# Strassen's scheme for the gate and up projections of a two-layer hybrid encoder on one NeuronCore

## The chip, the cores and the metric

One core of one Trainium2 chip runs the whole inference step as one program. The metric is device time in microseconds (us) of one execution; three runs of the kernel before gave 3285.12, 3286.22 and 3287.9 us. The core's engines run side by side and meet at semaphores: TensorE (PE, with PEld for its weight loads), VectorE (DVE), ScalarE (ACT), GpSimd (POOL) and SyncE (SP, which here issues weight loads). DMAs are issued from SP's and ACT's queues.

## The reference, cut to what matters

D is 1024, the feed-forward width D_FF is 2816, and 1024 prompt tokens and 32 sample tokens go together as N = 1056 columns. Each of the two layers ends in the part that the change touches:

```python
def _swiglu(h, wg, wu, wd):
    a = jnp.einsum('btd,df->btf', h, wg)
    b = jnp.einsum('btd,df->btf', h, wu)
    return jnp.einsum('btf,fd->btd', jax.nn.silu(a) * b, wd)
...
    xp = xp + g1p[:, None] * mp          # mp: the mixer's output projection
    hp = _modulate(xp, norm_ffn[l], sh2p, sc2p)
    xp = xp + g2p[:, None] * _swiglu(hp, w_ffn_gate[l], w_ffn_up[l], w_ffn_down[l])
```

`_modulate` is an RMSNorm with a gain, times (1 + scale), plus a shift. The other outputs (keys, values, states, of both layers) come from stages that the change leaves alone. All of it is float32.

## The kernel before, in words

Activations lie with features on the 128 partitions and tokens along the free dimension: `x` is [128, 8, 1056]. A float32 product is made of three passes (`passes`, L106 to L110): each operand is split into an upper part of fewer bits (`hi`, written as fp32r) and the rest (`lo`), and w_hi·hi, w_hi·lo and w_lo·hi are accumulated in PSUM. Who splits: GpSimd the weights (a CAST, L272, and a subtraction TENSOR_TENSOR, L274, over 2048 columns for a unit of two 128-wide weight blocks), ScalarE and VectorE the activations.

`trunk_phase` runs once for each layer. Its list of units (`TrunkPlan`) is: 4 "out" units (the mixer's output projection), then for each of six parts (4, 4, 4, 4, 3, 3 blocks of 128 features of D_FF) its "up" units and 4 "down" units, and in layer 0 at the end 8 "z" and 4 "tok" units, the next layer's input projection. An up unit is one block of gate and the same block of up. Every unit but tok goes over three thirds of 352 tokens, and for each third accumulates two PSUM banks (a = 0, 1) over k = 8 blocks (nk for down), three passes each: 24 matmuls a bank, 144 an up unit, 72 or 54 a down unit. There are three pairs of banks, reused in turn (`accumulator_free`).

After an up step, ScalarE takes Silu of the gate's bank (L357), VectorE multiplies by the up bank (L462), ScalarE writes the upper half (L359) and VectorE the rest (L466) to `inner`, from which the down units of the same part read. VectorE adds a down or out step to `x` (`residual`, L444). After the last out unit the norm of the feed-forward input is computed third by third, by `sums` on TensorE (L324), `roots` on ScalarE (L394) and `norm` on VectorE: a reciprocal (L482), then 8 tiles (L489), each shifted and split by ScalarE (L404) and `lower_half` (L473); the first up unit waits for them tile by tile (`h_ready`).

The order on each engine is written out by hand, by the list `events` and the loops over it; each engine runs its instructions in order. Weights come through two `raw` buffers: SP waits until GpSimd has split unit u - 2 before it loads unit u (the wait at L241), and GpSimd waits until TensorE has finished unit u - 2 before it writes w[u % 2].

## Time and profile before

| | us |
|---|---|
| median of three runs | 3286.22 |
| the profiled execution's own time | 3287.2 |
| its span in the trace | 3285.4 |
| TensorE busy | 3012.2 |
| VectorE, GpSimd, ScalarE busy | 1412.1, 846.2, 728.4 |
| trunk of layer 0, from the first out matmul to the last tok matmul | 933.0 to 2103.4 |
| trunk of layer 1, from the first out matmul to the last down matmul | 2389.2 to 3256.0 |

The profile is of one execution. Matmuls overlap in the pipe, so a matmul's own duration (322 ns at 352 columns) is twice the distance from one to the next (159 ns); the distance is what a matmul costs. Busy spans of GpSimd are rough.

### The profile page before, as it was taken

The numbers are of one execution on the slowest core, as the hardware profiler recorded it, in microseconds if no ns is written. First come the engines' busy times: TensorE is split into PE (matmuls) and PEld (weight loads), VectorE is DVE, ScalarE is ACT, GpSimd is POOL, SyncE is SP. The second block draws the span as 40 slices with busy tenths as digits, with TensorE's granted clock in tenths as the row PEclk, the third lists the DMA queues.
The fourth block names the chain that finished last, engine by engine and source line by source line (L and its number), as shares of the span: only waits on it lengthen the run. The fifth ranks groups of instructions, "written<-read, shape, count | busy, mean of one in ns | idle before, by whom it ended". The sixth has DMA issues, their size and how long they took to land. (4 is left out here: it accounts for less than half of the span.)

```text
span 3285.4 us, 55023 instructions
## 1 busy us (share of the span) xinstructions
PE 3012.2 (92%) x23527; PEld 2803.3 (85%) x23527; DVE 1412.1 (43%) x2792; ACT 728.4 (22%) x1659; POOL 846.2 (26%) x415
## 2 busy tenths in 40 slices
PE   6999999894769999999999999899689999999996
PEld 3859999562669999999999899766488999999996
DVE  5489999454647222122224400155347212122126
ACT  2341211453422100101002211266323010100102
POOL 1111222562422232222332222000032232232230
PEclk8999999996889999999999999999899999999998
DMA  5626662624051011110111222332120111011011
GB/s 200 220 78 217 224 226 81 210 81 135 3 203 39 27 58 46 46 58 26 49 54 53 76 99 75 117 137 102 45 101 27 52 39 65 26 58 46 28 56 61
DMA packets 135011, 290.89 MB, mean 89 GB/s; under 512 B 19032, under 2 KB 84336, under 8 KB 127152
## 3 DMA queue, kind: packets, MB, share of 16 engines
q1 hardware_dynamic: 104464, 244.87, 22.1%
q10 hardware_dynamic: 30304, 42.49, 3.6%
q8 instruction: 187, 3.06, 0.4%
q14 instruction: 56, 0.46, 0.0%
HBM read 244.51 MB, written 55.70 MB: 91 GB/s over the span
## 5 line engine op out<-in xcount | busy, mean ns | idle before, releaser
L108 PE MATMUL tr_acc<-tr_h_hi,tr_w_hi 128*128 128x352 f32 x2880 | 939.1, 326 | 69.4 <-POOL tr_w_lo L274 41.6
L109 PE MATMUL tr_acc<-tr_h_lo,tr_w_hi 128*128 128x352 f32 x2880 | 928.2, 322 | 0.0
L110 PE MATMUL tr_acc<-tr_h_hi,tr_w_lo 128*128 128x352 f32 x2880 | 927.5, 322 | 0.0
L108 PEld LDWEIGHTS tr_acc<-tr_h_hi,tr_w_hi 128*128 128x128 f32 x2880 | 544.1, 189 | 76.8 <-POOL tr_w_lo L274 42.1
L272 POOL CAST tr_w_hi<-tr_raw 128x2048 fp32r<-128x2048 f32 (+2 forms) x112 | 169.4, 1513 | 1543.8 <-PE tr_acc L110 1408.0
L109 PEld LDWEIGHTS tr_acc<-tr_h_lo,tr_w_hi 128*128 128x128 f32 x2880 | 545.7, 189 | 0.7
L110 PEld LDWEIGHTS tr_acc<-tr_h_hi,tr_w_lo 128*128 128x128 f32 x2880 | 544.2, 189 | 0.0
L274 POOL TENSOR_TENSOR tr_w_lo<-tr_raw,tr_w_hi 128x2048 fp32r<-128x2048 f32 (+2 forms) x112 | 405.5, 3620 | 9.0
L462 DVE TENSOR_TENSOR tr_value<-tr_value,tr_acc 128x352 f32<-128x352 f32 x132 | 68.7, 520 | 722.9 <-ACT tr_value L357 722.9
L444 DVE SCALAR_TENSOR_TENSOR x<-tr_acc,mod,x 128x352 f32<-128x352 f32 x448 | 194.6, 486 | 364.0 <-PE tr_acc L110 361.2
L108 PE MATMUL tr_acc<-tr_inner_hi,tr_w_hi 128*128 128x352 f32 x1056 | 342.2, 324 | 0.0
L109 PE MATMUL tr_acc<-tr_inner_lo,tr_w_hi 128*128 128x352 f32 x1056 | 339.4, 321 | 0.0
L110 PE MATMUL tr_acc<-tr_inner_hi,tr_w_lo 128*128 128x352 f32 x1056 | 338.9, 321 | 0.0
L357 ACT ACTIVATE tr_value<-tr_acc 128x352 f32<-128x352 f32 x132 | 61.2, 464 | 1185.8 <-PE tr_acc L110 1185.7
L560 DVE TENSOR_SCALAR_CACHE_REDUCE f_q<-score,choose_trial 128x384 bf16<-128x384 f32 (+6 forms) x224 | 242.2, 1145 | 1.1
L1488 DVE CUSTOM_DVE_ANT_0 pc_prob<-pc_dots,pc_bias 128x640 f32<-128x640 f32 (+4 forms) x128 | 83.2, 651 | 347.1 <-POOL pc_bias L1323 267.3
L108 PE MATMUL f_acc<-h_hi,f_w_hi 128*128 128x352 f32 x600 | 202.5, 337 | 7.2 <-DVE h_lo L1102 7.2
L109 PEld LDWEIGHTS tr_acc<-tr_inner_lo,tr_w_hi 128*128 128x128 f32 x1056 | 199.1, 189 | 0.4 <-issue 0.2
L108 PEld LDWEIGHTS tr_acc<-tr_inner_hi,tr_w_hi 128*128 128x128 f32 x1056 | 198.8, 188 | 0.4 <-DVE x L444 0.3
L110 PEld LDWEIGHTS tr_acc<-tr_inner_hi,tr_w_lo 128*128 128x128 f32 x1056 | 198.6, 188 | 0.0
L110 PE MATMUL f_acc<-h_hi,f_w_lo 128*128 128x352 f32 x600 | 193.4, 322 | 0.0
L109 PE MATMUL f_acc<-h_lo,f_w_hi 128*128 128x352 f32 x600 | 193.4, 322 | 0.0
(279 smaller groups left out, 4164.9 us busy)
## 6 DMA issues: line engine op xcount, KB each, us to landing
f_ada_w<-in_w_ada_dram SPq DMA_DIRECT2D x48, 1024.0 KB, 5.2
tr_raw<-in_w_gate_dram SPq DMA_DIRECT2D x44, 512.0 KB, 3.7
tr_raw<-in_w_up_dram SPq DMA_DIRECT2D x44, 512.0 KB, 4.5
tr_raw<-in_w_down_dram SPq DMA_DIRECT2D x64, 256.0 KB, 2.9
f_raw<-in_w_dram SPq DMA_DIRECT2D x24, 512.0 KB, 6.9
out_z_dram<-f_stage ACTq DMA_DIRECT2D x60, 176.0 KB, 1.9
out_z_dram<-tr_value ACTq DMA_DIRECT2D x48, 176.0 KB, 2.0
tr_raw<-in_w_out_dram SPq DMA_DIRECT2D x16, 512.0 KB, 8.3
```

The lines of the kernel that those rows point to most:

```text
L108: pe.matmul(out, w_hi, hi, start=start, stop=False)
L109: pe.matmul(out, w_hi, lo, start=False, stop=False)
L110: return pe.matmul(out, w_lo, hi, start=False, stop=stop)
L272: pool.tensor_copy(hi, own).then_inc(w_hi, 1)
L274: pool.tensor_tensor(lo, own, hi.bitcast(F32), ALU.subtract).then_inc(w_ready, 1)
L357: act.activation(value[n % 3][:], acc[s % 3][0][:, 0:THIRD], ACT.Silu).then_inc(gated, 1)
L444: done = dve.scalar_tensor_tensor(out=x[:, k, lo:hi], in0=acc[s % 3][a][:, lo - THIRD * t:hi - THIRD * t], scalar=gate[:, k, of:of + 1], i ...
L462: dve.tensor_tensor(value[n % 3][:], value[n % 3][:], acc[s % 3][1][:, 0:THIRD], ALU.mult).then_inc(multiplied, 1)
L560: last = dve.tensor_scalar(marks[n % 2][0:p, 0:width], score[0:p, at:at + width], bound(p, j), 0.0, compare, ALU.add, accum_out=count[0:p, ...
L1488: dve.tensor_tensor_reduce(prob[2 * (u % 3) + hd][:, 0:n], dots[hd][:, at_dots(u):at_dots(u) + n], add, -DH ** -0.5, 3.0e38, ALU.add, ALU. ...
```

## The change

The 8 products of a unit (2 halves of the tokens, 2 halves of the 1024 input features, gate and up) become 7 (Strassen's scheme in Winograd's form), with sums and differences of halves ahead and behind. Blocks of tokens are a quarter wide (264) and a half is 528. Per layer:

- Out units go over four blocks of 264 columns. Norm, shift and split of the feed-forward input go by halves of 528. Seven moving operands M1 to M7 of [128, 4, 528] are kept, each split into hi and lo (`quad`): three are quarters of the normed input, four are its differences (`full`).
- An up unit is seven products of 24 matmuls of 264 columns: 168. The first two units run as a pair, product by product, while the moving operands are being made, and compute M1 twice: 192 matmuls each.
- GpSimd makes four sums of the weight quarters (`combine`) and splits seven quarters of 512 columns (`factor`, `split`) for each up unit. Split weights go through a ring of six slots of a quarter unit.
- ScalarE and VectorE put gate and up together from the products (nine VectorE instructions and four of ScalarE, all of 528 columns, for each unit from the third on), the gated values are stored to DRAM, and after the last up unit all down units run; their inputs are loaded again and split (`part_half`, `part_rest`), two parts ahead at most.
- There are four pairs of PSUM banks.

```diff
+UP_ORDER = [M1, M2, M6, M5, M7, M3, M4]
+PAIR_ORDER = [M1, M2, M3, M5, M6, M7, M4]
+RING, RING_WIDE = 6, 8
...
-        self.units = [("out", j, 0, KD) for j in range(KD // 2)]
-        first, self.last_up = 0, {}
-        for nk in TRUNK_PARTS:
-            self.units += [("up", f, first, KD) for f in range(first, first + nk)]
+        self.units = [("out", j, 0, KD) for j in range(KD // 2)] + [("up", f, 0, KD) for f in range(KF)]
+        for first, nk in zip(PART_FIRST, TRUNK_PARTS):
             self.units += [("down", j, first, nk) for j in range(KD // 2)]
...
+            def split(u, n, own):
+                i = plan.slot_no[u, n]
+                hi, lo = slot(u, n)
+                width = own.shape[-1]
+                slot_free(i)
+                pool.tensor_copy(hi[:, 0:width], own).then_inc(w_hi, 1)
+                pool.wait_ge(w_hi, i + 1)
+                pool.tensor_tensor(lo[:, 0:width], own, hi[:, 0:width].bitcast(F32), ALU.subtract).then_inc(w_ready, 1)
+
+            def combine(u):
...
+                pool.tensor_tensor(w_sum[b][:], r21, r22, ALU.add).then_inc(combined, 1)
+                pool.wait_ge(combined, 4 * f + 1)
+                pool.tensor_tensor(r21, r11, r21, ALU.subtract).then_inc(combined, 1)
+                pool.wait_ge(combined, 4 * f + 2)
+                pool.tensor_tensor(r11, w_sum[b][:], r11, ALU.subtract).then_inc(combined, 1)
+                pool.wait_ge(combined, 4 * f + 3)
+                pool.tensor_tensor(r12, r12, r11, ALU.subtract).then_inc(combined, 1)
+                pool.wait_ge(combined, 4 * f + 4)
...
+            def half_sums(h):
+                pe.wait_ge(out_summed, add_no(UP_FIRST - 1, 2 * h + 1, 1) + 1)
...
+            def accumulate(u, n, product, out, start, stop):
+                f = u - UP_FIRST
+                pe.wait_ge(w_ready, plan.slot_no[u, n] + 1)
+                for b in range(2):
+                    for k in range(KH):
+                        if f == 0 and b == 0:
+                            pe.wait_ge(quad_ready, KH * QUADS[product] + k + 1)
...
+                        done = passes(pe, out[:, b, 0:BLOCK], w_hi_v, w_lo_v, upper, lower, start and k == 0, stop and k == KH - 1)
...
+            for j in range(UP_FIRST):
+                outputs(j)
+            pair_first(0)
+            half_sums(1)
+            pair_again(0)
+            pair_again(1)
+            pair_first(1)
+            for n in range(1, 7):
+                for f in range(2):
+                    pair_product(n, f)
+            for f in range(2, KF):
+                up_products(f)
...
+            def store_inner(f):
+                b, n = f % 2, f // 2
+                act.wait_ge(right_done[b], n + 1)
+                act.dma_start(io["inner"][f][:, HALF:N], flat(values_of(f)[1])).then_inc(right_stored[b], 16)
...
+            def unit_tile(h, k):
+                for lo, hi, s in HALF_SPANS[h]:
+                    own = slice(lo - HALF * h, hi - HALF * h)
+                    done = dve.scalar_tensor_tensor(out=full[2 * (k // KH) + h][:, k % KH, own], in0=x[:, k, lo:hi],
+                                                    scalar=up_gain[:, k, s:s + 1], in1=flat(rstd_half[h])[:, own],
+                                                    op0=ALU.mult, op1=ALU.mult)
...
+            def lower(product, k):
+                dve.wait_ge(quad_hi, KH * QUADS[product] + k + 1)
+                dve.tensor_tensor(quad[product][1][:, k], source[product][:, k], quad[product][0][:, k].bitcast(F32),
+                                  ALU.subtract).then_inc(quad_ready, 1)
+
+            def difference(n, k, out, first, second):
+                dve.tensor_tensor(full[out][:, k], full[first][:, k], full[second][:, k], ALU.subtract).then_inc(combo, 1)
...
+            for f in range(2, KF):
+                sum_gate_left(f)
+                sum_u2(f)
+                sum_u4(f)
+                sum_u3(f)
+                sum_up_right(f)
...
+                sum_gate_right(f)
+                right_product(f)
+                sum_up_left(f)
+                left_product(f)
...
+    dram("inner", [KF, P, N])
```

GpSimd's instructions before, for an up unit of layer 0 (2048 columns) and the two down units behind it: `raw0` and `raw1` are the loaded weights, `hi` and `lo` their split halves.

```order
L272 CAST tr0_w1_hi<-tr0_raw1 128x2048
L274 TENSOR_TENSOR tr0_w1_lo<-tr0_raw1,tr0_w1_hi 128x2048
L272 CAST tr0_w0_hi<-tr0_raw0 128x2x512
L274 TENSOR_TENSOR tr0_w0_lo<-tr0_raw0,tr0_w0_hi 128x2x512
L272 CAST tr0_w1_hi<-tr0_raw1 128x2x512
L274 TENSOR_TENSOR tr0_w1_lo<-tr0_raw1,tr0_w1_hi 128x2x512
```

From one up unit (the third of layer 0) in the changed kernel; `w_sum` holds one of the sums, `ring_hi` and `ring_lo` the slots.

```order
L409 CAST tr0_ring_hi_11284<-tr0_raw0_11282 128x512
L411 TENSOR_TENSOR tr0_ring_lo_11285<-tr0_raw0_11282,tr0_ring_hi_11284 128x512
L418 TENSOR_TENSOR tr0_w_sum0_11286<-tr0_raw0_11282 128x512
L420 TENSOR_TENSOR tr0_raw0_11282<-tr0_raw0_11282 128x512
L422 TENSOR_TENSOR tr0_raw0_11282<-tr0_w_sum0_11286,tr0_raw0_11282 128x512
L424 TENSOR_TENSOR tr0_raw0_11282<-tr0_raw0_11282 128x512
L409 CAST tr0_ring_hi_11284<-tr0_raw0_11282 128x512
L411 TENSOR_TENSOR tr0_ring_lo_11285<-tr0_raw0_11282,tr0_ring_hi_11284 128x512
L409 CAST tr0_ring_hi_11284<-tr0_w_sum0_11286 128x512
L411 TENSOR_TENSOR tr0_ring_lo_11285<-tr0_w_sum0_11286,tr0_ring_hi_11284 128x512
```

An up unit's two instructions of 2048 columns have become eighteen of 512: the first pair of rows stands twice ahead of L418, and the pair on `raw0` three more times behind the last row, so seven CASTs, seven subtractions and four sums.

VectorE at the opening of the up stage, before: `x` plus the last out step, then the norm's tiles.

```order
L482 RECIPROCAL tr_rstd<-tr_rstd 128x352
L489 SCALAR_TENSOR_TENSOR tr_tmp<-x,gains,tr_rstd 128x352 x2
L473 SCALAR_TENSOR_TENSOR tr_h_lo<-tr_tmp,mod,tr_h_hi 128x352
L489 SCALAR_TENSOR_TENSOR tr_tmp<-x,gains,tr_rstd 128x352
L473 SCALAR_TENSOR_TENSOR tr_h_lo<-tr_tmp,mod,tr_h_hi 128x352
```

The same stage in the changed kernel, from M5's operand to M6's: `full` are the quarters of the normed input and their differences, `quad` the split operands.

```order
L913 TENSOR_TENSOR tr_full_11247<-tr_full_11248,tr_full_11247 128x528
L909 TENSOR_TENSOR tr_quad_lo<-tr_full_11247,tr_quad_hi 128x528 x2
L913 TENSOR_TENSOR tr_full_11248<-tr_full_11250,tr_full_11248 128x528 x4
L913 TENSOR_TENSOR tr_full_11250<-tr_full_11250,tr_full_11247 128x528 x2
L909 TENSOR_TENSOR tr_quad_lo<-tr_full_11250,tr_quad_hi 128x528
L913 TENSOR_TENSOR tr_full_11250<-tr_full_11250,tr_full_11247 128x528
L909 TENSOR_TENSOR tr_quad_lo<-tr_full_11250,tr_quad_hi 128x528
```

Where the norm made 24 tiles of 352 columns, two instructions of VectorE each (three or four where a tile holds sample tokens), the opening now holds 16 tiles, 16 differences and 28 rests of 528 columns, all with two inputs in SBUF, ahead of and between the sums of the first two units.

## Rows read from the trace of the kernel before

**Rows 1.** The page's part 1: busy us, share of the span, instructions.

```profile
PE 3012.2 (92%) x23527; PEld 2803.3 (85%) x23527; DVE 1412.1 (43%) x2792; ACT 728.4 (22%) x1659; POOL 846.2 (26%) x415
```

**Rows 2.** Waits of PE, whole span: waited for, us in total, times, longest.

```profile
PE tr_acc L108 <- POOL tr_w_lo L274: 41.6, 2, 22.0
...
PE tr_acc L108 <- DVE tr_h_lo L473: 17.7, 6, 5.9
```

**Rows 3.** Windows: length, busy us (instructions) of PE, PEld, DVE, ACT, POOL, clock, DMA.

```profile
1062.00:1780.00 718.00, 716.57 (x4505) 716.29 (x4504) 176.80 (x339) 72.33 (x154) 205.34 (x86) 1.00 0.13 44
...
1200.00:1300.00 100.00, 100.00 (x631) 100.00 (x630) 21.37 (x36) 9.64 (x20) 27.08 (x12) 1.00 0.10 32
...
2005.00:2100.00 95.00, 95.00 (x804) 94.53 (x804) 0.00 (x0) 12.61 (x33) 16.13 (x5) 1.00 0.17 56
```

**Rows 4.** Waits of PE in the opening of up, layer 0 and then layer 1.

```profile
PE tr_acc L108 <- DVE tr_h_lo L473: 5.4, 2, 4.5
...
PE tr_acc L108 <- DVE tr_h_lo L473: 6.1, 2, 5.9
PE tr_acc L108 <- DVE tr_value L462: 1.9, 1, 1.9
```

**Rows 5.** Windows in the same opening of layer 0, as rows 3.

```profile
1038.00:1042.00 4.00, 0.46 (x1) 0.46 (x2) 4.00 (x4) 0.59 (x1) 2.62 (x1) 0.52 0.11 19
1042.00:1046.00 4.00, 4.00 (x17) 3.60 (x17) 3.77 (x9) 2.19 (x5) 0.00 (x0) 0.63 0.63 243
```

**Rows 6.** GpSimd's groups by shape: count, busy us, mean ns, idle before.

```profile
L274 POOL TENSOR_TENSOR tr_w_lo<-tr_raw,tr_w_hi 128x1024 fp32r<-128x1024 f32 x32 | 76.8, 2399 | 2.6
...
L272 POOL CAST tr_w_hi<-tr_raw 128x1024 fp32r<-128x1024 f32 x32 | 33.3, 1042 | 411.2 <-PE tr_acc L110 411.2
...
L1328 POOL TENSOR_TENSOR pa_extra<-pa_bias,score 128x512 f32<-128x512 f32 x8 | 10.0, 1273 | 2.9 <-DVE pa_least L1488 2.9
...
L272 POOL CAST tr_w_hi<-tr_raw 128x768 fp32r<-128x768 f32 x16 | 13.2, 827 | 191.9 <-PE tr_acc L110 191.9
```

**Rows 7.** Timeline of GpSimd at layer 1's start, and earlier: start, us.

```profile
2382.49 1.89 POOL L272 CAST tr_w_hi<-tr_raw 128x2048 fp32r<-128x2048 f32 x1 [98.78 <-DMA tr_raw<-in_w_out_dram]
2384.46 4.65 POOL L274 TENSOR_TENSOR tr_w_lo<-tr_raw,tr_w_hi 128x2048 fp32r<-128x2048 f32 x1
2389.06 2.18 POOL L272 CAST tr_w_hi<-tr_raw 128x2048 fp32r<-128x2048 f32 x1
2391.33 4.70 POOL L274 TENSOR_TENSOR tr_w_lo<-tr_raw,tr_w_hi 128x2048 fp32r<-128x2048 f32 x1
...
702.27 2.51 POOL L1328 TENSOR_TENSOR pa_extra<-pa_bias,score 128x512 f32<-128x512 f32 x2 [1.45 <-DVE pa_least L1488]
```

**Rows 8.** Timeline of VectorE beside it: start, us, count, idle before.

```profile
2385.94 5.68 DVE L503 TENSOR_TENSOR tr_h_lo<-tr_inner_hi,tr_h_hi 128x352 fp32r<-128x352 f32 x2 [1.19 <-ACT tr_h_hi L416]
2391.55 6.17 DVE L503 TENSOR_TENSOR tr_h_lo<-tr_inner_lo,tr_h_hi 128x352 fp32r<-128x352 f32 x4
...
2397.64 1.82 DVE L503 TENSOR_TENSOR tr_h_lo<-tr_inner_hi,tr_h_hi 128x352 fp32r<-128x352 f32 x4
```

**Rows 9.** Timeline in the up stage of layer 0: GpSimd, then VectorE.

```profile
1172.48 4.60 POOL L274 TENSOR_TENSOR tr_w_lo<-tr_raw,tr_w_hi 128x2048 fp32r<-128x2048 f32 x1
...
1174.22 1.08 DVE L444 SCALAR_TENSOR_TENSOR x<-tr_acc,mod,x 128x352 f32<-128x352 f32 x2 [2.49 <-PE tr_acc L110]
```

**Rows 10.** VectorE's groups by shape, as rows 6.

```profile
L462 DVE TENSOR_TENSOR tr_value<-tr_value,tr_acc 128x352 f32<-128x352 f32 x132 | 68.7, 520 | 722.9 <-ACT tr_value L357 722.9
...
L482 DVE RECIPROCAL tr_rstd<-tr_rstd 128x352 f32<-128x352 f32 x12 | 28.2, 2348 | 3.6 <-ACT tr_rstd L394 3.6
...
L489 DVE SCALAR_TENSOR_TENSOR tr_tmp<-x,gains,tr_rstd 128x320 f32<-128x320 f32 x24 | 13.1, 544 | 0.1
...
L489 DVE SCALAR_TENSOR_TENSOR tr_tmp<-x,gains,tr_rstd 128x32 f32<-128x32 f32 x24 | 5.9, 244 | 0.0
```

More of the change, by code:

```diff
@@ L126 @@
 assert sum(TRUNK_PARTS) == KF
+PART_FIRST = [sum(TRUNK_PARTS[:p]) for p in range(len(TRUNK_PARTS))]
 PART_MAX = max(TRUNK_PARTS)
@@ L172, in __init__ @@
         self.last_step = {u: s for s, (u, t) in enumerate(steps)}
-        counts, self.order = {"up": 0, "x": 0, "z": 0}, {}
+        counts, self.order = {"x": 0, "z": 0}, {}
         for u, t in steps:
-            group = {"out": "x", "down": "x", "tok": "z"}.get(self.units[u][0], self.units[u][0])
+            group = "x" if self.units[u][0] == "down" else "z"
             self.order[u, t] = (group, counts[group])
@@ L265, in _ @@
+            for u in range(DOWN_FIRST, len(units)):
+                kind, j, first, nk = units[u]
+                loaded(u)
                 if kind == "down":
-                    own, hi, lo = (blocks_view(v)[:, :, 0:nk] for v in (raw[b], w[b].hi, w[b].lo))
-                else:
-                    own, hi, lo = raw[b][:], w[b].hi[:], w[b].lo[:]
-                pool.wait_ge(w_in[b], 32 * (u // 2 + 1))
-                if u >= 2:
-                    pool.wait_ge(step_done, plan.last_step[u - 2] + 1)
@@ new lines, in matmuls @@
+                        if kind == "down" and j == 0 and t == 0 and a == 0:
+                            pe.wait_ge(part_ready, first + k + 1)
+                        if a == 0 and kind == "z" and j == 0:
+                            pe.wait_ge(h_ready, KD * t + k + 1)
+                        w_hi_v, w_lo_v = (v[:, P * (k % KH):P * (k % KH) + P] for v in slot(u, n))
+                        done = passes(pe, pair[s % 3][:, a, 0:THIRD], w_hi_v, w_lo_v, of_hi[:, k, lo:hi], of_lo[:, k, lo:hi],
+                                      k == 0, k == nk - 1)
@@ new lines, in matmuls, with sums @@
+                        if t == 2 and (k == nk - 1 or k % KH == KH - 1) and not (a and k == nk - 1):
+                            done.then_inc(mid, 1)
+                done.then_inc(step_done, 1)
+            def sums(t):
+                pe.wait_ge(summed, plan.sums_done[t])
+                if t >= 2:
+                    pe.wait_ge(root, t - 1)
+                pe.matmul(pair[3][:, t % 2, 0:THIRD], c.ones[:], total[t][:], start=True, stop=True).then_inc(ssq_ready, 1)
+            for j in range(UP_FIRST):
+                outputs(j)
@@ L329, in _ @@
                 elif what == "sum":
-                    sums(u, t)
+                    sums(t)
         @block.scalar
@@ new lines, in _ @@
+            half_roots(1)
+            for k in range(KH):
+                upper(M2, k)
+            for f in range(2):
+                keep_m1(f)
+            for k in range(KH):
+                shift_tile(1, KH + k)
+                upper(M3, k)
+            for k in range(KH):
+                shift_tile(1, k)
+            for k in range(KH):
+                upper(M5, k)
+            for f in range(2):
+                keep_m3(f)
+            for k in range(KH):
+                upper(M6, k)
@@ new lines, in _ @@
+            for k in range(KH):
+                lower(M2, k)
+            half_inverses(1)
+            for k in range(KH):
+                unit_tile(1, KH + k)
+                if k:
+                    lower(M3, k - 1)
+            lower(M3, KH - 1)
+            for k in range(KH):
+                unit_tile(1, k)
+            for k in range(KH):
+                dve.wait_ge(shifted, 3 * KH + k + 1)
+                difference(0, k, 0, 1, 0)
+                if k:
+                    lower(M5, k - 1)
```

752 lines of the change are left out of this document (615 added, 137 removed).

## The prediction, on record before the changed kernel ran

> **What bounds the kernel now.** I read the page's part 1 first: TensorE is busy for 92% of the span, so what counts is its own work and the few places where it waits [rows 1]. Then its waits over the whole span: in the trunk, 41.6 us for the first split weights of each layer and 17.7 us for tiles of a norm [rows 2]. Last the windows. Inside the trunk's long stretch TensorE is busy for 716.6 of 718 us at full clock, while VectorE has 177 us of work and GpSimd 205 [rows 3]. There only fewer or cheaper matmuls help, and the two others have three quarters of their time free. The change spends that free time, so the question is whether it lasts.
>
> **TensorE's own work.** The reader should take the distance of matmuls from the windows, not their durations: 100 us hold 631 matmuls of 352 columns, 0.1585 us each, and 95 us hold 804 of 256 columns, 0.1182 us each [rows 3]. Between the two, one column costs 0.0403 / 96 = 0.00042 us, so 264 columns cost 0.1182 + 8 x 0.00042 = 0.1216 us, very near a measured row; that is the value I take. Fewer columns do not pay in proportion, or it would be 0.1189. The weight loads hide at 256 columns too (PEld 94.5 of 95 us, yet the distance still fell), so 264 meets no floor of theirs. Bounds: 0.1189, and 0.1249 if a column above 256 costs twice that.
> Before, up is 2 x 22 x 144 = 6336 matmuls and out is 2 x 576 = 1152, together 7488 x 0.1585 = 1186.8 us. After, a unit is 7 x 24 = 168 and the first two of each layer are 192, so up is 2 x (20 x 168 + 2 x 192) = 7488, and out is 2 x 768 = 1536: 9024 x 0.1216 = 1097.3 us. The term is **-89.5 us** (bounds -114 and -60). One eighth fewer columns in up would be -126 us; a third of it goes in smaller matmuls, in M1 made twice and in the narrower out blocks. Down, z and tok keep their matmuls.
>
> **Who shares what.** GpSimd's subtraction of 2048 columns ran from 2384.46 to 2389.1; a VectorE TENSOR_TENSOR that began at 2385.94 and another behind it took 5.68 us, where four of them take 1.82 us on their own [rows 7, 8]. The first came right behind the subtraction, the second only behind the next CAST, which took 2.18 us where 1.89 is usual; four more, begun at 2391.55, took 6.17 us beside the next subtraction. So the two engines take turns, one instruction each. An instruction that reads PSUM and one SBUF tile is not held up: two took 1.08 us in the midst of a subtraction [rows 9]. The CAST behind a VectorE instruction grew by 0.29 us, not by the whole 0.455.
> The Trainium skill, page "SBUF — State Buffer", section "Who interferes with whom", has the rule: a VectorE instruction with two SBUF inputs and a GpSimd instruction that reads SBUF exclude each other, and the later one blocks until the other is through. By that rule alone each turn costs the whole instruction, which gives the upper end of the next term; the trace shows a tenth of a microsecond less for each turn.
>
> **The opening of up**, in each layer, from the end of out block 1 of the last out unit to the end of the pair's M4. TensorE's own work there: two out blocks 2 x 48 x 0.1216 = 11.7, four small sums 1.8, 16 products of 24 x 0.1216 = 2.92 us: 46.7; together 60.2 us.
> VectorE: 352 columns cost 0.455 us in a row [rows 8], a column 0.00104 us (544 less 244 ns over 288 columns, [rows 10]), so 528 columns cost 0.64. With two SBUF inputs: 54 TENSOR_TENSOR (28 rests, 16 differences, 10 sums and products) 34.6 us, 8 tiles at 0.68 5.4, 8 tiles in two pieces (496 + 32) at 0.82 6.6, four small sums 1.5: 48.1 us. Without: two reciprocals at 2.35 x 1.5 = 3.5 us, two residuals 2.3 and six sums from PSUM at 0.52 + 0.18 = 0.70 us [rows 10]: 13.5 us. In all 61.6 us. It starts some 5 us into the window (residual, square, sum, root), and waits about 3 us for ScalarE.
> GpSimd: a subtraction of 512 columns costs 1.27 us, 1.24 from start to start (2.51 us for two) [rows 6, 7]; a CAST 1.042 - 0.215 x 2 = 0.61, plus the 0.07 that stand between CAST and subtraction; a link of the chain of sums 1.34. In this window it has 16 slots at 1.92 (M2 of the pair up to M7 of the third unit's run ahead) and 12 sums: 30.7 + 16.1 = 46.8 us.
> If the two never meet, VectorE ends at 5 + 61.6 + 3 = 70 us: ten behind TensorE's 60. If every turn costs in full, at 5 + 61.6 + 3 + 46.8 = 116. I take the turns as the trace has them: GpSimd passes beside VectorE's 13.5 + 3 us of other work, and about 50 turns save 0.1 us each: 5 + 61.6 + 3 + 46.8 - 16.5 - 5 = 95 us. TensorE then waits 35 us a layer. Before, it waited 5.4 us in layer 0 and 8.0 in layer 1 [rows 4] and ran some 8 us behind that wait at 0.52 to 0.63 of its clock (1.2 GHz for the most part, against 2.4), worth about 2.5 us [rows 5]: 9 us on average. The term is 2 x (35 - 9) = **+52 us** (bounds 0 and 2 x (56 - 9) = +94).
> Each such wait, of 5 us and more, lets the clock fall as in rows 5. Where VectorE is last that costs nothing; behind the first M1 and at the last M4 it does: **+6 us** for both layers (0 to 12).
>
> **The steady up units.** TensorE's period is 168 x 0.1216 = 20.4 us. GpSimd's: seven CASTs at 0.68, six subtractions at 1.24, the seventh and the four sums at 1.34 because each waits for the one before: 4.8 + 7.4 + 6.7 = 18.9 us. Four of VectorE's nine instructions have two SBUF inputs (u4, up right and the two products) and take 0.29 x 1.5 = 0.43 us of GpSimd's time each: 20.6 us. That is 0.2 a unit more than TensorE. It starts the stretch with about four slots ready (11.7 us), of which half must stay as cover for the four sums, so 6 us a layer may be lost free of charge and 20 x 0.2 = 4 are: no wait. I take 2 us a layer for uneven turns, **+4 us**. Bounds: 0, and with GpSimd's reported durations, gaps of 0.14 and whole turns: 7 x 0.75 + 11 x 1.41 + 4 x 0.64 = 23.3 us, (20 x 2.9 - 12) x 2 = +92.
> On such durations the Trainium skill, page "Perfetto Trace Analysis", section "GPSIMD Engine Instruction", says to time GpSimd by the spacing of starts and not by the span reported. Rows 7 bear it out: a span of 4.65 and the next start 4.60 us later. By spans without gaps the period is 18.2 + 1.7 = 19.9 us, by starts 20.6: TensorE would be the bound by the one and not quite by the other.
> VectorE needs 4 x 0.64 + 5 x 0.70 = 6.1 us and up to four waits of 1.3; its results are wanted at least three products (8.8 us) later, as four pairs of banks go round. ScalarE's four instructions and two stores fit in likewise. They cost nothing while TensorE or GpSimd is late by itself.
>
> **The rest.** First weights: the first quarter is split 5 us sooner, but TensorE then stands before the mixer's tiles, which it also did (3.4 us); 0, bounds -4 and +4. Gated values: 12 MB stored and 12 MB loaded, against 0.13 of the DMA engines in use [rows 3]; the loads of the first down part start with five products (15 us) to go; SP's later weight loads stand behind them and are not due before the first down unit's 11 us are over: 0, up to +10. ScalarE and VectorE split 1056 columns about each 2.9 us of down, beside free time.
>
> **Sum.** -89.5 + 52 + 6 + 4 = -27.5 us. The profiled execution took 3287.2 us (span 3285.4), so 3259.7; the median of runs is 1 us lower: **3259 us**.
>
> **The rivals.**
> A, the forecast: VectorE and GpSimd, in turns, set the opening; GpSimd keeps pace behind it. 3259, own range 3235 to 3285. Chance 0.5.
> B, turns are rare, because GpSimd is stopped by full slots when VectorE is busiest. The opening costs what it did: 3286 - 89.5 = 3197, with 3197 to 3225 for a few turns. For it: the slots free only as TensorE advances. Against: 46.8 us of GpSimd's work fall due in that window whatever its order. Chance 0.2.
> C, GpSimd becomes the bound of the twenty units: slower than before. Place: the 18 instructions of a unit; it decides from a period of 21.0 us (20.4 + 12 / 20), and at 23.3 gives 3259 + 88 = 3347. For it: my period is 20.6. Against: the start-to-start rows. Chance 0.15.
> D, the opening costs the full turns, the clock low for much of it: -89.5 + 94 + 6 + 4 = +14.5, 3301; with part of it the sum is nothing, 3286. Chance 0.15.
> That the products are not fewer is ruled out by the changed order: 3744 up matmuls a layer, all of 264 columns.
>
> **Chances.** What a measurement of this kernel can tell from no change is about 0.2%, 6.6 us. Faster: 0.46 of A and B, 0.66. Same: 0.04 of A, 0.05 of D, 0.02 of C, 0.11. Slower: the rest of C and D, 0.23. The range of 3200 to 3310 leaves out the far part of C and a little of B.
>
> **What would show it.** The spacing of 264-column matmuls: 0.1216. In the opening: waits of TensorE for `quad_lo`, `kept` and `full`, some 35 us a layer in chunks of 5 us and more; VectorE's two-input instructions at 1 to 2 us beside GpSimd, its sums from PSUM at 0.7; the window near 95 us. In the steady units: TensorE busy over 97% and a period of 20.4 to 20.8 us. I am wrong if waits for `ring_lo` recur in each unit (C), or if VectorE is busy for less than 70 us of the opening (B).

## The result, and the profile after

The changed kernel takes 3240.88 us (median of four runs, 3238.75 to 3244.22) against 3285.67 us for the kernel before on the same chip: a ratio of 0.9864, 95% interval 0.9847 to 0.9881. It is 44.8 us faster, where 27 were forecast. The profiled execution took 3238.75 us, its span is 3236.6; against the profiled run of before (3287.2) that is 48.5 us less. One execution of the run without the four sums (3791.6 us) and one of the run with twice the traffic (3453.88 us) were slow ones, at a lower granted clock, and are left out of the medians below.

The page's part 1, to be laid beside [rows 1]:

```profile
PE 2932.1 (91%) x25067; PEld 2723.5 (84%) x25067; DVE 1669.7 (52%) x3016; ACT 792.5 (24%) x1689; POOL 1481.0 (46%) x1335
```

TensorE has 80 us less work, VectorE 258 us more, GpSimd 635 us more. Then the windows inside the long stretch of up, beside [rows 3]: length, busy us (instructions) of PE, PEld, DVE, ACT, POOL, clock, DMA.

```profile
1140.00:1500.00 360.00, 360.00 (x2969) 360.00 (x2967) 140.24 (x159) 44.03 (x70) 343.67 (x315) 1.00 0.22 79
...
2560.00:2940.00 380.00, 380.00 (x3133) 380.00 (x3132) 150.17 (x169) 47.22 (x75) 362.66 (x334) 1.00 0.22 78
```

360 us hold 2969 matmuls of 264 columns, 0.1213 us each; counted from start to start, without the matmuls that lie across the window's ends, it is 0.1214. TensorE never stands, and GpSimd has gone from a quarter of the time to 95% of it. The waits of PE for the trunk's tiles, whole span, beside [rows 2]:

```profile
PE tr_acc L108 <- POOL tr_ring_lo L411: 33.6, 3, 17.8
...
PE tr_acc L108 <- DVE tr_kept L940: 16.2, 2, 8.2
PE tr_acc L108 <- DVE x L881: 15.6, 2, 7.8
...
PE tr_acc L494 <- DVE tr_kept L892: 12.4, 2, 6.5
PE tr_acc L108 <- ACT tr_kept L688: 10.7, 2, 6.1
```

The first row is the wait for the first weights, in the place of `tr_w_lo`. The four others are new and stand in the opening of up, once in each layer. They took the place of the 5.4 and 8.0 us of [rows 4] (layer 0 had 1.4 us more before, for `tr_value`).

The two traces laid side by side, stage by stage, in us:

| stretch | before | after | difference |
| --- | --- | --- | --- |
| layer 0's trunk, `eps` memset to the last tok matmul | 1184.7 | 1156.3 | -28.4 |
| layer 1's trunk, memset to the end of the span | 910.8 | 893.5 | -17.3 |
| first memset to first matmul, layer 0 / 1 | 14.0 / 14.6 | 9.9 / 10.3 | -4.1 / -4.3 |
| all else (code that isn't changed) | 1189.9 | 1186.8 | -3.1 |

The last line is no effect of the change: the first memset fell at 912.4 to 920.0 us in fourteen traces, over the same code. Another profiled run of the changed kernel had 1158.7 and 893.5 us for the two trunks.

**The turns in the opening.** Timeline of GpSimd and VectorE in layer 0 of the changed kernel, merged by start: start, us, engine, line, operation.

```profile
1029.36 1.72 POOL L418 TENSOR_TENSOR tr_w_sum<-tr_raw 128x512 f32<-128x512 f32 x1
1029.88 1.76 DVE L902 SCALAR_TENSOR_TENSOR tr_full<-x,gains,tr_kept 128x528 f32<-128x528 f32 x1
1031.16 1.62 POOL L420 TENSOR_TENSOR tr_raw<-tr_raw 128x512 f32<-128x512 f32 x1
1031.57 3.46 DVE L909 TENSOR_TENSOR tr_quad_lo<-tr_full,tr_quad_hi 128x528 fp32r<-128x528 f32 x2
1032.85 1.61 POOL L422 TENSOR_TENSOR tr_raw<-tr_w_sum,tr_raw 128x512 f32<-128x512 f32 x1
1034.54 1.61 POOL L424 TENSOR_TENSOR tr_raw<-tr_raw 128x512 f32<-128x512 f32 x1
```

Read the starts: GpSimd's last three sums begin 1.69 us apart, and VectorE's three instructions end 1.7 us apart as well. Each engine gets one instruction in a turn of 1.69 us, though GpSimd's takes 1.29 alone and VectorE's 0.71. VectorE's instructions report both their own time and the wait for the other; GpSimd's grow too, by 0.3. The turn is shorter than the two durations together (2.00), and shorter than the two distances from start to start when each works alone (1.36 between two sums, 0.62 between two of VectorE's, together 1.98): the instructions of a turn overlap by 0.3 us.

**GpSimd's pace in the steady units.** The same sum in the fourth and in the last up unit, and ScalarE's copy of M1, which follows TensorE's first product of each unit:

```profile
1126.11 1.29 POOL L418 TENSOR_TENSOR tr_w_sum<-tr_raw 128x512 f32<-128x512 f32 x1
...
1497.47 1.28 POOL L418 TENSOR_TENSOR tr_w_sum<-tr_raw 128x512 f32<-128x512 f32 x1
```

```profile
1118.32 0.61 ACT L681 ACTIVATE tr_kept<-tr_acc 128x528 f32<-128x528 f32 x1 [3.93 <-PE tr_acc L110]
...
1505.67 0.61 ACT L681 ACTIVATE tr_kept<-tr_acc 128x528 f32<-128x528 f32 x1 [4.44 <-PE tr_acc L110]
```

Eighteen units of GpSimd take 371.4 us, 20.63 each; nineteen of TensorE 387.4 us, 20.39 each. GpSimd is the slower of the two by 0.24 us a unit and lives on its stock of ready pieces, which lasts: TensorE needs 20.39 us for every one of the twenty units in both layers.

**The passage to z.** The prediction has no term for it. Before, VectorE's last norm began beside splits of 2048 columns:

```profile
1809.43 4.67 POOL L274 TENSOR_TENSOR tr_w_lo<-tr_raw,tr_w_hi 128x2048 fp32r<-128x2048 f32 x1
1809.65 4.83 DVE L489 SCALAR_TENSOR_TENSOR tr_tmp<-x,gains,tr_rstd 128x352 f32<-128x352 f32 x1
```

After, the pieces have 512 columns, and two of them are split before the norm begins. Behind them GpSimd stands for 38.5 us, until TensorE frees a slot, so that all but the first of the norm's instructions meet none of GpSimd's:

```profile
1777.82 1.26 POOL L411 TENSOR_TENSOR tr_ring_lo<-tr_raw,tr_ring_hi 128x512 fp32r<-128x512 f32 x1
1778.88 1.08 DVE L1056 SCALAR_TENSOR_TENSOR tr_tmp<-x,gains,tr_rstd 128x352 f32<-128x352 f32 x2
...
1817.60 0.61 POOL L409 CAST tr_wide_hi<-tr_raw 128x512 fp32r<-128x512 f32 x1 [38.52 <-PE tr_acc L110]
```

Before, 42 of the products' matmuls start between 1796 and 1820 us, 6.7 us of work in 24; after, 51 start between 1774 and 1790, 8.1 us in 16. So 17 us were lost there before, and 8 after.

### The profile page after: what moved, and what is told of

It is laid out like the page before. It is cut to its first block and busy times, and to the rows that moved or that the text cites. A ratio compares the mean times of both kernels' runs of the same rounds, so it can differ in the third digit from the quotient of the medians.

```text
span 3236.6 us, 59936 instructions
## 1 busy us (share of the span) xinstructions
PE 2932.1 (91%) x25067; PEld 2723.5 (84%) x25067; DVE 1669.7 (52%) x3016; ACT 792.5 (24%) x1689; POOL 1481.0 (46%) x1335
## 5 line engine op out<-in xcount | busy, mean ns | idle before, releaser
L108 PE MATMUL tr_acc<-tr_quad_hi,tr_ring_hi 128*128 128x264 f32 x2496 | 720.3, 289 | 46.9 <-DVE tr_kept L940 16.2
L110 PE MATMUL tr_acc<-tr_quad_hi,tr_ring_lo 128*128 128x264 f32 x2496 | 716.5, 287 | 0.0
L109 PE MATMUL tr_acc<-tr_quad_lo,tr_ring_hi 128*128 128x264 f32 x2496 | 715.5, 287 | 0.0
L411 POOL TENSOR_TENSOR tr_ring_lo<-tr_raw,tr_ring_hi 128x512 fp32r<-128x512 f32 (+1 forms) x428 | 562.9, 1315 | 34.2
L108 PEld LDWEIGHTS tr_acc<-tr_quad_hi,tr_ring_hi 128*128 128x128 f32 x2496 | 477.5, 191 | 49.4 <-DVE tr_kept L940 16.6
L109 PEld LDWEIGHTS tr_acc<-tr_quad_lo,tr_ring_hi 128*128 128x128 f32 x2496 | 477.8, 191 | 0.2
L110 PEld LDWEIGHTS tr_acc<-tr_quad_hi,tr_ring_lo 128*128 128x128 f32 x2496 | 477.5, 191 | 0.0
L108 PE MATMUL tr_acc<-tr_part_hi,tr_ring_hi 128*128 128x352 f32 x1056 | 341.7, 324 | 1.8 <-DVE x L1022 1.4
L109 PE MATMUL tr_acc<-tr_part_lo,tr_ring_hi 128*128 128x352 f32 x1056 | 339.1, 321 | 0.0
L110 PE MATMUL tr_acc<-tr_part_hi,tr_ring_lo 128*128 128x352 f32 x1056 | 338.9, 321 | 0.0
```

Source lines behind the costliest of these rows:

```text
L108: pe.matmul(out, w_hi, hi, start=start, stop=False)
L109: pe.matmul(out, w_hi, lo, start=False, stop=False)
L110: return pe.matmul(out, w_lo, hi, start=False, stop=stop)
L411: pool.tensor_tensor(lo[:, 0:width], own, hi[:, 0:width].bitcast(F32), ALU.subtract).then_inc(w_ready, 1)
```

## The experiments

Each run has its own runs of the kernel before beside it on the same chip; times below are medians, ratios are to the kernel before. The theory is that of turns: a VectorE instruction with two SBUF inputs and a GpSimd instruction get in one after the other, one instruction at a time, and this sets the opening. The stretch of the opening is taken from the end of out block 1 to the third unit's first matmul. The main rival is that the opening is a chain of VectorE's and ScalarE's own work, whatever GpSimd does.

**The changed kernel again.**

> The changed kernel once more, as the reference of the runs beside it. Every theory: 3238 to 3245 us, 0.985 to 0.988 of the kernel before.

3240.75 us, 0.9866 (0.9852 to 0.9879). It is the reference for the versions of it below.

**GpSimd out of the way in the opening.** It splits and sums 16 of the 512 columns, so the pair's products use stale weights.

```diff
-                width = own.shape[-1]
+                width = 16 if n and UP_FIRST <= u < UP_FIRST + 2 else own.shape[-1]
...
+                wide = 16 if f < 2 else KH * P     # the pair's four sums as well
```

> The changed kernel, but GpSimd splits and sums only 16 of the 512 columns of the pair's weights (all of them behind the two first M1 pieces), so the pair's products use stale weights; TensorE, VectorE and ScalarE do the same work. Theory of turns (the opening of up is as long as VectorE's two-SBUF-input instructions and GpSimd's instructions laid end to end): some 30 us of GpSimd's 46.8 us in the opening go, VectorE no longer stands behind them, the opening shrinks by 10 to 18 us a layer: 3205 to 3221 us, VectorE's two-input instructions back at about 0.7 us. Rival (the opening is the chain residual, square, root, reciprocal, norm, split, and ScalarE's part in it, whatever GpSimd does): 3236 to 3242 us.

3206.49 us, 0.9757 (0.9742 to 0.9772): 34 us less. The longest waits of PE in the opening of layer 0, and VectorE's differences, whose mean was 908 ns in the changed kernel:

```profile
PE tr_acc L108 <- DVE x L884: 3.6, 1, 3.6
PE tr_acc L108 <- ACT tr_kept L691: 3.6, 1, 3.6
PE tr_acc L108 <- DVE tr_kept L943: 2.9, 1, 2.9
```

```profile
L916 DVE TENSOR_TENSOR tr_full<-tr_full,tr_full 128x528 f32<-128x528 f32 x32 | 21.0, 702 | 0.0
```

The opening takes 81.8 and 81.4 us in the two layers, where the changed kernel has 99.5 and 100.3. The four long waits of layer 0 are 2.5 to 6 us shorter each, 13 us in all where it was 30.7. The rival is ruled out: TensorE, VectorE and ScalarE had the same instructions in the same order.

**Another order in the opening.**

```diff
-                if n == 1:
-                    combine(UP_FIRST)
-                    combine(UP_FIRST + 1)
+            for n in range(1, 4):      # right behind the first M1 piece
+                link(first, n)
...
-            for f in range(2):
-                add_m5(f)
-            for f in range(2):
-                sum_u2(f)
-                sum_gate_right(f)
+            sum_u2(0)                  # behind the rests of M7
...
+            sum_u2(1)
```

> The changed kernel, all results kept: five of the pair's eight weight sums move ahead into GpSimd's idle 13 us in front of the opening; VectorE splits the tiles of M7 before the last four differences and releases the banks (u2) right behind the M6 products; ScalarE keeps the first M3 product before the upper tiles of M5. Theory of turns: five turns of about 1.1 us fewer on VectorE's path, and 3 us from u2 coming sooner: 6 to 8 us a layer, 3225 to 3233 us. Rival (VectorE's own work sets the opening, and order moves only where the wait stands): 3237 to 3242 us.

3241.75 us, 0.9868 (0.9855 to 0.9882): nothing. PE's waits, layer 0:

```profile
PE tr_acc L108 <- DVE tr_kept L977: 9.0, 1, 9.0
PE tr_acc L108 <- DVE x L896: 7.8, 1, 7.8
PE tr_acc L108 <- DVE tr_quad_lo L924: 5.4, 6, 2.0
```

The wait for u2 (L940 in the changed kernel, 8.0 us) is now one for u3 (L977, 9.0 us). VectorE works from 1071 to 1108 us with no break that its timeline shows; I take it that what it does first therefore does not matter to what comes last. In front, M2's rests began 3.3 us sooner (1047.56 instead of 1050.88); at the end the third unit began no sooner (the opening takes 100.1 and 101.7 us), and GpSimd's splits and sums for that unit (1089 to 1107 us) fell between VectorE's instructions as before. My expectation counted the turns taken away at one place and not that others come in their stead.

**The kernel before, with GpSimd's splits in four pieces.**

```diff
-                pool.tensor_copy(hi, own).then_inc(w_hi, 1)
+                for n in range(4):
+                    own, hi, lo = (blocks_view(v)[:, n // 2, k0:k1] for v in (raw[b], w[b].hi, w[b].lo))
+                    pool.tensor_copy(hi, own).then_inc(w_hi, 1)
...
-                    pe.wait_ge(w_ready, u + 1)
+                    pe.wait_ge(w_ready, 4 * (u + 1))
```

> The kernel before (eight products), but each weight unit of 2048 columns is split in four pieces of 512 by GpSimd; TensorE still waits for the whole unit. Nothing else changes, so the weights come no sooner. Theory of turns (a VectorE instruction with two SBUF inputs waits out the whole GpSimd instruction, 4.7 us for 2048 columns and 1.3 for 512): the passage from down to z (16 us lost before, 7 after) gives 5 to 9 us, the two layer openings and the tail 2 to 8 together: 3268 to 3280 us. Rival (the passage got shorter because the first quarter of the z weights is ready sooner, not because of the turns): 3285 to 3289 us, the small gaps between 8 instructions instead of 2 being hidden.

3276.30 us, 0.9971 (0.9961 to 0.9981), 9.7 us less with eight products still. Layer 0's trunk took 1176.6 us (8.0 less), layer 1's 909.3 (1.5 less), though the first matmul came 1.5 and 2.1 us later after the memset. The norm of the z passage, beside the row of 4.83 us above:

```profile
1799.81 1.43 POOL L275 TENSOR_TENSOR tr_w_lo<-tr_raw,tr_w_hi 128x512 fp32r<-128x512 f32 x1
1800.03 1.59 DVE L490 SCALAR_TENSOR_TENSOR tr_tmp<-x,gains,tr_rstd 128x352 f32<-128x352 f32 x1
```

So the kernel before gains over 9 us by the size of the pieces alone, by shorter turns. By the traces, 4.1 and 2.3 us of it lie in the two layers' out units and 4.0 in the passage to z with the z units. The changed kernel gained 9.0 us in that passage: there GpSimd stood beside the norm, here it still splits beside it, and the first pairs of VectorE's instructions take 2.36 us each instead of 0.99. So the size of the pieces is less than half of that gain; that the rest comes from GpSimd's standing still is read from the two traces and was not tried apart.

**The same, and TensorE starts at the first piece.**

```diff
+                        if t == 0 and kind in ("out", "z") and k % 4 == 0:
+                            pe.wait_ge(w_ready, 4 * u + 2 * a + k // 4 + 1)
```

> As the kernel before with splits in four pieces of 512 columns, and TensorE also starts a unit of out or z at its first piece instead of the fourth. Theory of turns alone: as with pieces alone, 3268 to 3280 us, within 2 us of it. Theory that earlier first weights count as well: another 2 to 5 us a layer at the start of out (TensorE's first product 5 us sooner, its clock up sooner) and 1 to 4 at z: 5 to 12 us less than with pieces alone, 3258 to 3274 us.

3275.29 us, 0.9967 (0.9954 to 0.9979). The first matmul comes 9.4 and 10.0 us after the memset instead of 15.5 and 16.6, and the time is the same: TensorE then waits another 3.7 and 2.6 us for the mixer's tiles, at half its clock. Earlier first weights are worth nothing there, as the prediction had it.

**Less and more work for GpSimd in the steady units.** First without its four sums there (the products then use other weights):

```diff
                 factor(u, 0)
                 factor(u, 1)
-                combine(u)
```

> The changed kernel without GpSimd's four weight sums in the twenty steady up units of a layer (their products use other weights). Forecast (TensorE is the bound there, GpSimd's 19.5 of 20.4 us a unit are hidden): no change in the steady stretch, at most 1 to 3 us a layer in the opening, where the third unit's sums stood in VectorE's way: 3235 to 3242 us. Rival (GpSimd already holds TensorE up now and then): 3200 to 3230 us.

3240.38 us, 0.9862 (0.9847 to 0.9877): no change. The window beside the one above:

```profile
1140.00:1500.00 360.00, 360.00 (x2968) 360.00 (x2967) 156.15 (x159) 44.10 (x70) 243.57 (x248) 1.00 0.22 79
```

100 us of GpSimd's work less, and the same matmuls. Then with one sum more:

```diff
+                more(u)        # w_sum = r21 + r22, once more
                 combine(u)
```

> The changed kernel with one more weight sum of 512 columns in each steady up unit (the first one made twice). GpSimd is busy 19.45 of 20.37 us a unit; with 1.3 us more, 0.1 for the gap: 20.9, above TensorE's 20.4. Forecast: 0.5 us a unit for 20 units less a stock of some 6 us, 4 to 10 us a layer: 3249 to 3261 us, with waits of TensorE for ring_lo. If GpSimd's gaps held more slack than it seems: 3239 to 3245 us. If it was the bound already: 40 x 1.4 = 56 us more, 3297 us.

3299.47 us, 1.0041 (1.0028 to 1.0053): 59 us more. ScalarE's copy of M1 in two units that follow each other, and PE's waits:

```profile
1426.69 0.61 ACT L689 ACTIVATE tr_kept<-tr_acc 128x528 f32<-128x528 f32 x1 [4.44 <-PE tr_acc L110]
1448.78 0.61 ACT L689 ACTIVATE tr_kept<-tr_acc 128x528 f32<-128x528 f32 x1 [4.44 <-PE tr_acc L110]
```

```profile
PE tr_acc L108 <- POOL tr_ring_lo L412: 79.6, 34, 18.1
```

A period of 22.1 us, and 43.6 us of the 79.6 are waits of 1.5 us at most in the steady units, 15 in each layer. They do not begin at once: in both layers the first four units still take 20.39 us each, the fifth 20.62, and only the last fifteen 22.09. The stock covered the deficit of 1.7 us of nearly five units, some 8 us. My 20.9 us was wrong in its base: I took GpSimd's busy time (19.45 us a unit) for its period and the rest for slack. The rest is the gaps between its 18 instructions, and they don't give way. From the starts, 20.63 + 1.46 = 22.1 would have come out. The two runs together place the changed kernel: on TensorE's side of the edge, with a deficit of 20 x 0.24 = 4.8 us against a stock worth some 8.

**The detour through DRAM, with twice the traffic.**

```diff
+                act.dma_start(io["spare"][0][f], io["w_up"][l][f]...).then_inc(spare_in[0], 16)
...
                     sp.dma_start(staged[:, k], io["inner"][f]).then_inc(part_in[k], 16)
+                    sp.dma_start(io["spare"][1][f], io["w_gate"][l][f]...).then_inc(spare_in[1], 16)
```

> The changed kernel with the traffic of the detour through DRAM about doubled: each stored unit also issues a copy of 512 KB from DRAM to DRAM on ScalarE's queue, each reloaded one another on SyncE's. Forecast (the detour is hidden): 3238 to 3245 us. Rival (the round trip holds up the passage from up to down, or its traffic slows the weight loads): 5 to 20 us more, 3246 to 3262 us.

3254.21 us, 0.9909 (0.9894 to 0.9924): 14 us more, where no change was forecast and 5 to 20 us were the rival's. The loss stands where up passes into down. PE's waits there, layer 0, then layer 1:

```profile
PE tr_acc L108 <- DVE x L1027: 6.0, 1, 6.0
...
PE tr_acc L108 <- POOL tr_ring_lo L413: 6.8, 1, 6.8
```

In the changed kernel the same stretch has a single wait of 0.4 us in layer 0 and one of 1.4 in layer 1. In layer 0 it is a residual that comes late: on VectorE it stands behind the rests of reloaded tiles, which wait 5.4 us for ScalarE's upper halves, where it was 1.65. In layer 1 it is the weights. The steady units kept their 20.39 us each. So the detour as it is costs next to nothing that a wait shows, but at the first down units it has no room for twice the traffic. The extra copies take places in the queues as well as bandwidth; which of the two counts stays open.

**Fewer, wider instructions on VectorE.** On top of the other order, 10 instructions in the place of 32 for the differences and for the rests of M5, M6, M7 and M4. The last differences now also stand ahead of M6's rests, and u3 of the first unit comes sooner:

```diff
-            for k in range(KH):
-                dve.wait_ge(combo, 2 * KH + k + 1)
-                difference(3, k, 2, 2, 3)
+            dve.wait_ge(combo, 3 * KH)
+            differences(3, 0, KH, 2, 2, 3)      # one instruction of 2112 columns
```

> All results kept. The kernel with the opening reordered, in which the reorder alone gave nothing; now VectorE's 16 differences are 5 instructions instead (up to 2112 columns) and the rests of M5, M6, M7 and M4 are 5 instead of 16, and the first u3 comes ahead of the second pair of right sums. VectorE's columns and GpSimd's instructions stay the same. Theory of turns by the instruction (each VectorE instruction with two SBUF inputs lets one GpSimd instruction in, whatever its length): 22 fewer turns of which about half meet a GpSimd instruction, 1.0 us each, 8 to 12 us a layer: 3218 to 3228 us. Rival (it is the two engines' total time that adds up, however cut): only 22 x 0.09 us of fixed cost, and 2 us a layer from u3: 3234 to 3240 us.

3229.35 us, 0.9827 (0.9814 to 0.9841): 12 us less than the order alone: between the two accounts, 1 us off the theory's range and 5 off the rival's. VectorE's groups, and a split of GpSimd between them:

```profile
L929 DVE TENSOR_TENSOR tr_quad_lo<-tr_full,tr_quad_hi 128x2112 fp32r<-128x2112 f32 x6 | 16.0, 2661 | 5.6 <-ACT tr_quad_hi L689 5.6
L933 DVE TENSOR_TENSOR tr_full<-tr_full,tr_full 128x2112 f32<-128x2112 f32 x6 | 15.9, 2650 | 0.4
```

```profile
1085.77 3.27 POOL L412 TENSOR_TENSOR tr_ring_lo<-tr_raw,tr_ring_hi 128x512 fp32r<-128x512 f32 x1
```

2112 columns take 2.65 us in one piece in the mean (2.34 with no GpSimd instruction beside them, 3.24 behind a subtraction), where four differences of 528 took 4 x 0.908 = 3.63 in the changed kernel. The bill goes to GpSimd: its subtraction now takes 3.27 us instead of 1.3, and in the opening it can afford that.

The opening itself got 10.3 and 10.8 us shorter than with the order alone (89.8 and 90.9 us instead of 100.1 and 101.7), which is inside the theory's 8 to 12 us a layer and far from the rival's 4. Some of it was given back behind the opening. TensorE's last wait (2.7 and 3.4 us) now stands right before the third unit, which runs its first matmuls at 1.2 GHz and takes 21.8 and 22.0 us instead of 20.39. And in layer 0 the last five units take 20.75 us each: GpSimd's stock ran out. What the changed order of these instructions adds was not tried apart from their width.

**The second root early.** The same for M1 and M2, and the last out block's residual and sums ahead of them.

```diff
-            pair_first(0)
             half_sums(1)
+            pair_first(0)
...
-            for k in range(KH):
-                lower(M2, k)
+            lowers(M1, 0, KH)
...
+            lowers(M2, 0, KH)
```

> All results kept. The same with wide VectorE instructions for M1 and M2 as well, and VectorE and ScalarE take the last out block's residual, squares and root ahead of the M1 and M2 tiles, so that VectorE no longer stands 3.5 us before the second root. Theory of turns: six more turns gone and 3 us less of standing: 3 to 7 us a layer below the kernel with wide instructions for M5 to M4, 3206 to 3222 us. If M1's rests in one piece come so late that TensorE's idle time there grows into the path: no gain over it or up to 6 us lost.

3222.54 us, 0.9804 (0.9791 to 0.9818), 7 us less, half a us above the range that was expected. Little of it is the opening: 89.4 and 89.3 us, 0.4 and 1.6 less. In layer 0 another 2 us come from the last steady units, which are back at 20.39 us each, and in layer 1 2.7 us lie in the out units, where runs of the same code differ by up to 3. So this run does not show what six turns fewer are worth.

**The left sums first.** TensorE still stood 3.4 us before the third unit.

```diff
+            sum_up_left(0)
+            right_product(0)
+            sum_up_left(1)
+            right_product(1)
             for f in range(2):
-                right_product(f)
-            for f in range(2):
-                sum_up_left(f)
                 left_product(f)
```

> All results kept. The kernel with wide VectorE instructions and the early second root, in which TensorE stood 3.4 us before the third unit because VectorE made the two right products (3.5 us) ahead of the left sum that frees the banks; here each left sum comes first. Forecast: 2 to 3.5 us a layer less, 3215 to 3219 us. Rival (the third unit then waits for GpSimd's pieces, or the pair's M4 for a sum delayed in exchange): 3221 to 3224 us, the same as before this edit.

3231.24 us, 0.9830 (0.9816 to 0.9843): 9 us slower, although the wait is gone and the opening is 3.2 and 3.4 us shorter. Here is the main part of why: ScalarE's copy of M1 at the end of up, in two units that follow each other.

```profile
1482.06 0.61 ACT L696 ACTIVATE tr_kept<-tr_acc 128x528 f32<-128x528 f32 x1 [4.44 <-PE tr_acc L110]
1502.80 0.61 ACT L696 ACTIVATE tr_kept<-tr_acc 128x528 f32<-128x528 f32 x1 [4.44 <-PE tr_acc L110]
```

20.74 us a unit, in place of 20.39. GpSimd's period is the same 20.74 us (from 1186.42 to 1497.51 us, fifteen units). TensorE, no longer late, had eaten up GpSimd's stock after two units; the other eighteen take 20.73 us each in both layers, the time being lost before the third product, whose weights are the first piece behind the four sums. GpSimd sets the pace: rival C of the prediction, come true by way of a gain elsewhere. The sum by the traces, a layer: -3.3 for the opening, -1.5 because the first unit no longer starts at 1.2 GHz, +6.3 for the pace. That is +1.5 net, of the 3.5 us a layer that the traces show. Another 3.4 us in layer 0 and 0.8 in layer 1 were lost where up passes into down, where a wait of 2.1 us for a residual is new in layer 0; what makes it late was not looked into.

**VectorE takes over one of the four sums.**

```diff
                 link(u, 3)
-                link(u, 4)
+                if u == UP_FIRST + 2:
+                    link(u, 4)
...
+                if f < KF - 1:
+                    last_link(f + 1)       # VectorE: r12 - r11
```

> All results kept. The kernel in which the third unit starts 3.9 us earlier, but where the steady units then took 20.73 us each instead of 20.39; now VectorE makes the last of the four weight sums from the fourth unit on, so GpSimd has 17 instructions a unit instead of 18. Theory (with TensorE no longer late, GpSimd's own 20.7 us a unit had become the bound, its stock of ready pieces being used up): GpSimd's period falls to about 20.73 - 1.4 + 0.4 = 19.7 us, the steady period returns to TensorE's 20.39, and the earlier start stays won: 3 us a layer below the kernel without the earlier start, 3213 to 3219 us. Rival (the longer period came from a bank or from VectorE, which now has one instruction more): 3228 to 3236 us, period 20.7 or longer.

3212.35 us, 0.9777 (0.9763 to 0.9790): 19 us under the run before, 28 under the changed kernel, 73 under the kernel before, with all results kept. All units but the first of each layer (20.51 us) are back at 20.39 us. The window from 1150 us:

```profile
1150.00:1500.00 350.00, 350.00 (x2885) 350.00 (x2885) 166.39 (x173) 43.41 (x69) 331.63 (x298) 1.00 0.23 81
```

Without the shared sum these 350 us held 2837 matmuls. GpSimd now waits for free slots again, 3.4 us in all of this window, where it had waited for nothing. The opening takes 86.1 and 85.9 us.

## Why the prediction was right, step by step

**The forecast as a whole.** Rival A was the likeliest and it came: turns in the opening, GpSimd keeping pace behind. 3240.9 us lies in its own range (3235 to 3285), 18 us below the point. The mechanism was right; the size was short by more than a third, and inside the opening two errors cancelled.

**Streaming.** Forecast 0.1216 us for 264 columns, measured 0.1214 from start to start. Going between the distances at 256 and 352 columns was good to 0.2%. The distances before were read a little low, since a window's count takes in matmuls that lie across its ends: from start to start the 352-column matmuls stand 0.1589 us apart and not 0.1585. 9024 x 0.1214 less 7488 x 0.1589 is -94.3, so the term was 5 us larger than -89.5.

**The opening.** Forecast: a stretch of 95 us, 35 us of waits and 3 for the clock in each layer. Measured: 99.5 and 100.3 us, with 30.7 and 28.6 us of waits, and PE's own 60.2 us; that leaves 8.6 and 11.5 us, of which 5.9 and 8.6 are matmuls that ran at 1.2 GHz (60 and 88 of them, 0.22 us each). The sum, 39.3 and 40.1 us lost, was forecast as 38; its parts were not, and that the sum came out is partly luck. In layer 0:

```profile
1032.00:1036.00 4.00, 0.12 (x1) 0.12 (x1) 3.91 (x5) 1.60 (x4) 3.84 (x3) 0.67 0.00 0
1036.00:1040.00 4.00, 4.00 (x18) 4.00 (x19) 3.90 (x4) 0.68 (x2) 3.77 (x4) 0.50 0.00 0
...
1044.00:1048.00 4.00, 0.56 (x1) 0.50 (x2) 3.22 (x7) 1.47 (x3) 3.02 (x3) 0.50 0.00 0
1048.00:1052.00 4.00, 4.00 (x22) 3.65 (x21) 1.12 (x2) 2.39 (x5) 0.00 (x0) 0.70 0.00 0
```

Behind each of the long waits TensorE works at 1.2 GHz: 18 matmuls in 4 us instead of 33. I had said that this costs nothing where VectorE is last. VectorE is last, but not always: it stood for 11.6 and 12.3 us of the opening, where I had 8. How much of what the slow matmuls cost came to stand on the path no run here tells apart. That the turns set the stretch is shown by the run that took them away (81.8 us), and by the run that made them fewer (89.8). A turn with one of the sums saved 0.3 us, where I had taken 0.1.

The Trainium skill, page "SBUF — State Buffer", section "Who interferes with whom", says that a VectorE instruction with two SBUF inputs and a GpSimd instruction that reads SBUF stand in each other's way, and that the order of issue decides which of them blocks. The traces agree, both ways: with 2112 columns on VectorE it is GpSimd's subtraction that takes 3.27 us. That the wait lasts until the other is wholly through they do not bear out to the last tenth, with turns of 1.69 us for instructions of 1.29 and 0.71.

**The steady units.** Forecast: GpSimd 20.6 us a unit, TensorE 20.4, the deficit paid from GpSimd's stock. Measured: 20.63 and 20.39. I charged 2 us a layer for uneven turns; it was 0. Rival C was nearer than its chance of 0.15 says: an opening 3.3 us shorter than the best one without it brings it. The busy time alone misleads: 343.67 / 360 x 20.39 = 19.5 us a unit, and yet GpSimd is the slower engine. To time GpSimd from start to start, as the Trainium skill's page "Perfetto Trace Analysis", section "GPSIMD Engine Instruction", says, gave the right figure.

**The rest.** First weights 0: right, by the run with quarters. Gated values 0: right, with less room than I thought.

**What was missing.** The two traces laid side by side gained 45.7 us in the trunks (28.4 and 17.3), 18 more than the 27.5 of the forecast. Stage by stage, with each stage's own matmuls taken off, measured less forecast:

| | us, both layers |
| --- | --- |
| streaming | -5 |
| passage to z, layer 0 alone | -9 |
| from the memset to out block 1 | -4.5 |
| steady units | -4 |
| opening, with what it cost before | +1 |
| up into down | +2.5 |

The sum is -19, so that about 1 us stays open. The third line scatters: in the other profiled run of the changed kernel it is -2.4. The kernel before with splits in four pieces gained 4.1 and 2.3 us there too, so shorter turns are its likely cause. The passage to z is the place that my list of costs did not have: I priced turns where the change added work, and not where the old instructions met long ones of GpSimd. The rows named the place. Of the 17.7 us that TensorE waited for `tr_h_lo` [rows 2], 5.4 and 6.1 are the two openings [rows 4]; the other 6.2 stand at this passage. The row of 5.68 us in [rows 8] is a turn of the same kind, in front of out. Layer 1's trunk, which has no z, gained 17.3 us, nearer to the 13.7 a layer forecast.

## What to carry to other kernels

Where two engines take turns, count the turns: the price of one instruction is up to the length of the other engine's instruction, so cut the instructions of the engine that has time into small pieces and make those of the engine that is late few and wide. Compare a helper's period from start to start with the bound engine's period, never its busy share, and ask before speeding up the way into a long steady stretch whether the helper's stock was what covered its deficit. Measure stage by stage, from start to start: a gain at one place can be real and be given back at the next, and the total shows only the difference. In the one run that tried it by itself, a new order moved a wait and did not shorten it, in a stretch where one engine works without a break.

## What was not expected of the hardware

GpSimd's gaps are no slack: busy for 343.7 of 360 us, its period rose from 20.63 to 22.09 us with one more sum, 1.46 us for an instruction of 1.29 us alone. A VectorE instruction of 2112 columns with two SBUF inputs holds a GpSimd subtraction of 512 columns up for 2 us (3.27 instead of 1.3), while VectorE loses less than a subtraction's length (2.76 us beside it against 2.34 alone). And a kernel got 9 us slower by losing a wait of 3.4 us, of which some 4 us, behind the up units, have no explanation.
